# Short runs of extra matmuls at TensorE's longest waits, in a two-block transformer kernel on one core

## What is computed

```python
# mixer of layer 1 ("stick"): 16 heads, per query block
z = einsum('bhqd,bhkd->bhqk', qb, kb) * scale
log_stay  = where(causal, log_sigmoid(-z), 0.0)
log_after = cumsum(log_stay, axis=3, reverse=True) - log_stay
weights   = where(causal, exp(log_sigmoid(z) + log_after), 0.0)
out       = einsum('bhqk,bhkd->bhqd', weights, vb)

# second block, per layer; mixer 0 is NSA (three branches: compressed,
# selected, window), mixer 1 is forgetting attention ("fox")
h = rms_norm_2(x, norm_g[i, 0])
m = nsa_mixer(h, ...) if i == 0 else fox_mixer(h, ...)
x = x + rms_norm_2(m, norm_g[i, 1])                                  # post norm
h = rms_norm_2(x, norm_g[i, 2])
x = x + rms_norm_2(squared_relu_mlp(h, w_up[i], w_down[i]), norm_g[i, 3])  # post norm
```

## Time and profile before

| | |
|---|---|
| three runs | 1797.10, 1798.36 and 1802.62 us; median 1798.36 us |
| profiled execution, first to last instruction | 1802.1 us |
| TensorE busy | 1713.9 us, 95% of that span |
| VectorE, ScalarE, GpSimd busy | 1078.2, 789.6, 193.4 us |
| mean TensorE clock granted | 0.970 of 2.4 GHz |
| read from HBM | 280 MB, 156 GB/s over the span |
| chain of work that ended last | TensorE 86%, VectorE 6%, ScalarE 4% of the span |

### The profile page before, as it was taken

The page is one execution under the profiler, slowest core; times in us unless marked ns, Lnnn a source line. Parts: engine busy times, 40 slices in busy tenths (PEclk is TensorE's granted clock), DMA queues, the critical chain, the costliest instruction groups (busy, mean ns, idle before and its releaser), DMA issues.

```text
span 1802.1 us, 30970 instructions
## 1 busy us (share of the span) xinstructions
PE 1713.9 (95%) x13150; PEld 1644.2 (91%) x13150; DVE 1078.2 (60%) x1034; ACT 789.6 (44%) x903; POOL 193.4 (11%) x141
## 2 busy tenths in 40 slices
PE   7999998999999999999999999888999899789997
PEld 7999985899999999989999988677999898679997
DVE  7555776465567655676556776555655565456553
ACT  6343466444345434454344434434444443344441
POOL 1000123200002000120001351212000011120000
PEclk9999999999999999999999998789999999899999
DMA  7554451264453554455544442011655343125540
GB/s 294 187 187 162 176 201 44 74 237 183 167 187 149 202 210 164 163 201 191 209 164 163 183 178 94 24 57 68 227 178 176 136 164 140 71 76 205 186 163 24
DMA packets 39631, 282.26 MB, mean 157 GB/s; under 512 B 4416, under 2 KB 4544, under 8 KB 5760
## 3 DMA queue, kind: packets, MB, share of 16 engines
q1 hardware_dynamic: 39168, 279.59, 41.9%
q0 software_dynamic: 384, 1.51, 0.2%
HBM read 280.03 MB, written 1.05 MB: 156 GB/s over the span
## 4 chain that ended last, share of the span: by engine, by line
PE 86%; DVE 6%; ACT 4%; DMA 1%; POOL 1%; issue 1%; POOLq 0%; SPq 0%; ACTq 0%; DVEq 0%
PE ps L326 26%; PE ps L327 26%; PE ps L328 26%; DMA raw<-weights 1%; DVE hT_lo L1181 1%; ACT arena L1031 1%; ACT w_hi L873 1%; PE ps L656 1%; DVE w_lo L1169 1%; PE ps L600 1%; PE ps L408 1%; DVE arena L1273 1%; PE ps L613 1%; PE ps L632 0%; PE ps L657 0%
## 5 line engine op out<-in xcount | busy, mean ns | idle before, releaser
L326 PE MATMUL ps<-hT_hi,w_hi 128*128 128x256 f32 x2520 | 722.7, 287 | 32.0 <-DVE hT_lo L1181 26.2
L327 PE MATMUL ps<-hT_lo,w_hi 128*128 128x256 f32 x2520 | 717.1, 285 | 0.0
L328 PE MATMUL ps<-hT_hi,w_lo 128*128 128x256 f32 x2520 | 716.8, 284 | 0.0
L1169 DVE TENSOR_TENSOR w_lo<-raw,w_hi 128x2048 fp32r<-128x2048 f32 x264 | 600.6, 2299 | 136.7 <-ACT w_hi L873 136.6
L873 ACT ACTIVATE w_hi<-raw 128x2048 fp32r<-128x2048 f32 x264 | 494.8, 1902 | 67.2 <-DMA raw<-weights 67.1
L326 PEld LDWEIGHTS ps<-hT_hi,w_hi 128*128 128x128 f32 x2520 | 487.2, 193 | 36.1 <-issue 16.8
L327 PEld LDWEIGHTS ps<-hT_lo,w_hi 128*128 128x128 f32 x2520 | 488.1, 194 | 0.8 <-issue 0.7
L328 PEld LDWEIGHTS ps<-hT_hi,w_lo 128*128 128x128 f32 x2520 | 487.8, 194 | 0.0
L326 PE MATMUL ps<-hid_hi,w_hi 128*128 128x256 f32 x1256 | 355.7, 283 | 2.1 <-DVE hid_lo L1237 2.1
L327 PE MATMUL ps<-hid_lo,w_hi 128*128 128x256 f32 x1256 | 356.6, 284 | 0.0
L328 PE MATMUL ps<-hid_hi,w_lo 128*128 128x256 f32 x1256 | 351.6, 280 | 0.0
(11 more groups left out here) (222 smaller groups left out, 1451.8 us busy)
## 6 DMA issues: line engine op xcount, KB each, us to landing
raw<-weights SPq DMA_DIRECT2D x264, 1024.0 KB, 4.8
X<-x SPq DMA_DIRECT2D x2, 512.0 KB, 7.0
out<-X SPq DMA_DIRECT2D x4, 256.0 KB, 2.0
arena<-p POOLq DMA_DIRECT2D x2, 256.0 KB, 5.4
arena<-counts POOLq DMA_DIRECT2D x1, 512.0 KB, 5.3
arena<-nsa_tables POOLq DMA_DIRECT2D x1, 448.0 KB, 7.0
const<-constants SPq DMA_DIRECT2D x1, 423.0 KB, 9.7
cols<-parameters SPq DMA_DIRECT2D x1, 213.5 KB, 2.6
```

Of the source, the lines that this page charges most:

```text
L326: nc.tensor.matmul(dst, a_hi, b_hi, start=start, stop=False, skip_group_check=True)
L327: nc.tensor.matmul(dst, a_hi, b_lo, start=False, stop=False, skip_group_check=True)
L328: return nc.tensor.matmul(dst, a_lo, b_hi, start=False, stop=stop, skip_group_check=True)
L1169: nc.vector.tensor_tensor(unit_cols(w_lo, u, 0, UNIT), raw[:, r * UNIT:(r + 1) * UNIT], f(unit_cols(w_hi, u, 0, UNIT)), ALU.subtract).then ...
```

## The change

A helper `keep_clock(n, b)` issues n matmuls of 128 x 512 from `hid_hi` into bank b. Their result is read by nobody, and no semaphore counts them. It is called

- behind `spread(3)` in `post_norm`: 16 into bank 1, four times in the program;
- ahead of the wait of `weighted(g)` in stick: 14 into bank 7 for g = 0, 8 into bank 0 for g = 1 and 2, 4 into bank 0 for g = 3;
- ahead of the wait for the transposed weights in NSA's `weighted(n)` of each cmp job: 8 into bank 4;
- in `compress`, behind the wait for bank 2 and ahead of that for the hidden values: 8 into bank 2.

That is 64 + 34 + 32 + 8 = 138 matmuls. Since bank 0 is written now, the wait for `z_used`, which was not needed before, stands ahead of weighted(1).

```diff
+            def keep_clock(n, b):
+                for _ in range(n):
+                    nc.tensor.matmul(bank(b), hid_hi[:, 0:P], hid_hi[:, 0:512], start=True, stop=True, skip_group_check=True)
...
             def post_norm(first):
                 sum_squares(range(first, 4), 3)
                 spread(3)
+                keep_clock(16, 1)
...
                 def weighted(g):
+                    if g:
+                        keep_clock(8 if g < GROUPS - 1 else 4, 0)
+                    else:
+                        keep_clock(14, 7)
                     pe.wait_ge(*w_ready.due(me))
...
                 for n in range(GROUPS):
+                    if n == 1:
+                        pe.wait_ge(*z_used.due(me))
                     weighted(n)
                     if n + 2 < GROUPS:
                         after(n + 2)
-                z_used.due(me)
                 project(u0 + 12)
...
+                    if br == "cmp":
+                        keep_clock(8, 4)
                     pe.wait_ge(*tA_done.due(me))
...
                 def compress():
                     pe.wait_ge(*s_used.due(me))
+                    keep_clock(8, 2)
                     pe.wait_ge(*hid_cmp.due(me))
```

## The result

| | before | changed |
|---|---|---|
| runs | 20 | 20 |
| median | 1799.28 us | 1805.59 us |
| lowest to highest | 1796.75 to 1807.94 us | 1801.96 to 1807.49 us |

The ratio of the two is 1.0026, with a 95% interval of 1.0017 to 1.0034: 3 to 6 us slower, where 0.0 was forecast. It is not the quotient of the medians, which lie 6.3 us apart; it stands for 4.7 us. That is inside the 0.3% that the prediction called no measurable change, but only by the width of this 0.3%: the interval leaves 1 out, and the median lies 1.1 us above the upper end of the predicted range. The kernel became slightly slower, and the sum that gave 0.0 did not see it.

The account below looks back on a forecast made before the run. TensorE was busy 95% of the span, so time at 1.2 GHz on the path was in question. Terms -0.7, 0, -0.4, -0.8, +0.8, +1.4, 0 and -0.3 summed to 0.0: 1798.4 us forecast, range 1790.5 to 1804.5.

Parts of the forecast that it names:

- Falls that move: NSA's cmp jobs: clock falls move to new waits, 0 to +1.4 us for each of three head groups, taken +0.8 in all.
- Job 5, -0.8: NSA's cmp job 5: 2.3 us of its wait stay empty; bounds 0 and -2.5 us, taken -0.8.
- the surest term: NSA's job 11: added matmuls delay the weighted sum that project needs, +1.4 us on the path, +3.2 at 1.2 GHz.
- Stick, -0.7: Stick: after(3) may lose up to 3.7 us, weighted(3) win up to 1.4; taken +0.7 and -1.4, so -0.7.
- Compress, 0: NSA's compress: gain goes into job 0's wait and 11 us at clock 0.50 stay; 0, or up to -5 us.
- the post norms, 0, 0, 0 and -0.3: Behind NSA, fox and the last post norm 0; behind the first MLP bounds 0 and -1.4 us, taken -0.3.
- The price of a matmul: Each added matmul: 0.23 us from start to start at 2.4 GHz, at most 0.46 at 1.2 GHz.
- the clock holds in every wait up to 3.3 us: Rival, chance 0.19: gains in stick, jobs 2, 5, 8 and fox, less job 11, sum to -7.1 us, so 1791.3.
- the added matmuls run at 1.2 GHz: Rival, chance 0.11: also the clock falls ahead of after(3); +9.5 us less 1.4 for weighted(3), about 1806.5.

Follow-up runs that it names:

- before again: The kernel before, unchanged, run once more against the kernel before: 1799.39 us beside 1798.69, ratio 1.0010.
- the filled NSA kernel: Kernel before plus all of the change's NSA matmuls and ten more ahead of each of weighted(3), (6) and (9): 1799.20 us beside 1799.33, ratio 1.0000.
- with NSA filled the part as made: Kernel before plus NSA's matmuls without job 11's, ten ahead of weighted(3), (6), (9), and stick's 14, 8, 8, 4: 1796.59 us beside 1798.67.
- the whole change with both fills: The whole change plus ten matmuls ahead of each of weighted(3), (6), (9) and twelve ahead of after(3): 1796.24 us beside 1799.07 before, ratio 0.9987.
- the fastest kernel: Kernel before plus NSA's matmuls without job 11's, stick's matmuls, ten ahead of weighted(3), (6), (9), twelve ahead of after(3): 1795.19 us beside 1799.07.
- the stick kernel with its fill: Kernel before plus stick's 14, 8, 8 and 4 matmuls and twelve more ahead of after(3): 1802.86 us beside 1799.33, ratio 1.0012.
- the kernel without the stick part: Kernel before plus NSA's matmuls without job 11's, and ten ahead of each of weighted(3), (6) and (9): 1797.63 us beside 1799.07, ratio 0.9994.

## Why the prediction was off, by its own steps

**Falls that move: the step that failed.** The mechanism was forecast and is there: a wait of about 3 us without matmuls ahead of weighted(3) and weighted(9), with the clock at 0.50 behind it. Its price was set at +0.8 us for three head groups. Against before again they cost 1.64, 1.65 and 1.76 us on the path; two of them win 0.14 and 0.15 ahead of it, so 4.8 net. NSA as a whole grew by 6.1 us (102.2 to 108.3), which with 1.3 for job 11 leaves the same 4.8. The kernel with these matmuls alone measured +3.3, against -0.4 for the same terms in the sum (-0.4 - 0.8 + 0.8). The bound of +1.4 for each fell short by 0.2 to 0.4, since it counted the weighted sum alone, and the clock stays down over the first transposes behind it; the value taken in it was far too small. The row on which I costed it is only a part of the reason. In that execution of before, weighted(3) stood at 1.2 GHz nearly to its end, where in before again half of its work runs at full speed. But even against that execution weighted(3) and (9) cost 1.27 and 1.47 us more with the change, and (6) 0.48 less: +2.3 in all, and not +0.8.

**Job 5, -0.8.** In the profile of before the clock was down from 1158.2 to 1171.8, over weighted(6), and against it the change does win 1.05 us from weighted(5) to (6) (8.37 to 7.32). In before again the clock was back at 1163.6, and that distance is 7.30: there was nothing to win.

**The base.** I knew that the profiled span lay 3.7 us over the median (5.6, with the 1.9 between a span and its run's time), subtracted that, and went on reading its rows as if the surplus lay evenly. It lay in NSA, at the place that the change touches: half of the 7.5 us from the first scores to weighted(1), where the clock was down for 17 us and not 10.2, and 3.2 us around weighted(6). The page's row of the clock, too, shows 7 or 8 only in NSA's slices and one of fox, not at stick and the post norms, as the prediction has it.

**Job 11, "the surest term", +1.4.** In the trace the weighted sum follows the transposes' start by 2.2 us and not by 0.9, so +1.3. It is 1.3 again in the trace of the kernel with job 11's alone. That kernel measured +0.7, with an interval of 0.9996 to 1.0018 that holds both 0 and 1.4; leaving it out took 1.6 us from the filled NSA kernel (1799.20 to 1797.63, in two series). The size is borne out, not more.

**Stick, -0.7.** By itself +2.5, which looked like a failed step. But its section was no longer than in before again (33.4, 33.7 and 32.1 us from after(1)'s last matmuls to `project` in the three traces that have it as made, against 33.8), and with NSA filled the part as made measured 2.1 us under before, where the kernel without it measured 1.4 under: -0.7, with intervals of two us on either side this doesn't confirm the forecast, but it makes +2.5 as a cost of its own unlikely. The two halves are as costed: after(3) lost (5.9 us against 3.67; in the kernel before run again, which had a fall there too, 5.3), weighted(3) won (from 3.6 to 2.2 us). One of the prediction's signs of being wrong, after(3) near 6 us, thus came. Here too the profile was of the rarer kind: of the eight traces in which stick is unchanged, six have after(3) at 5.2 to 6.7 us and a section of 33.4 to 33.8, and two, that profile among them, 3.67 us and 31.6 to 31.8. So the sum charged the change with a fall that most executions had already. Where the 2.5 us of the stick part alone were lost, its one trace does not show: it is of one of the fastest executions (1797.73 us), with 102.3 us for NSA.

**Compress, 0, and the post norms, 0, 0, 0 and -0.3.** Right against before again: the gain of compress went whole into job 0's wait, and from the first scores to weighted(2) it is 33.7 us with the change and 33.8 in before again. But the 11 us at 0.50 did not stay, as the prediction had it; the clock was down for 3.4 us there, and against the profile of before that distance shrank by 3.7. Behind NSA's post norm the gain went into the wait for POOL's squares, 1.56 where about 1.7 was forecast. Behind the first MLP the clock fell between the chunks, as feared. From `spread(3)` to the next stage's `spread(7)` it is 19.7 us behind NSA and fox and 22.4 behind the first MLP, in before again and with the post norms' matmuls alone: nothing was won. The four together measured +0.3.

**The price of a matmul** was 0.23 us, as forecast: sixteen take 3.90 us and eight 2.11, so that eight more take 1.8. A whole set takes 0.2 to 0.6 us more than its number times 0.23, as its row reaches from the first start to the last modelled end. At 1.2 GHz, where one set ran in the whole change with both fills, eight took 3.78 us, 0.43 from start to start, where at most 0.46 was forecast.

**The rivals.** That the clock holds in every wait up to 3.3 us is ruled out by the windows. That the added matmuls run at 1.2 GHz is ruled out too at stick, jobs 2 and 11, though its other half, the fall ahead of after(3), came true, and its time of 1806.5 lies nearest to the 1805.59 measured. It came there for another reason.

**What stays open.** Why NSA takes its longer course more often after the stick part is not shown. The runs show two groups of times, one trace of before in each, and a lower granted clock in the upper one. That the shorter stick moves NSA against whatever times the clock's changes is an inference from these; no execution of the stick kernels from the upper group was profiled. Nor does the difference simply go once NSA's waits are filled: NSA with its next waits filled still spreads from 1796.1 to 1804.6 us, and in the trace of the fastest kernel NSA began 4.5 us earlier than in that of the kernel without the stick part (1093.31 and 1097.80) and took 4.9 us longer (106.15 and 101.28). A second cause stands beside the clock and was not tested, a transfer. In the stick kernel with its fill NSA began 4.5 us earlier than in before again and ended only 1.8 earlier, in an execution of the lower group; 2.0 of the 2.7 us lie ahead of job 0's transposes, and there the last weights to be rounded ahead of NSA's masks came 1.3 us later, counted from NSA's first scores (ScalarE's rows, first the stick kernel with its fill, whose first scores are at 1093.41, then before again, at 1097.95):

```profile
1093.78 1.91 ACT L862 ACTIVATE w_hi<-raw 128x2048 fp32r<-128x2048 f32 x1 [5.07 <-DMA raw<-weights]
```

```profile
1096.98 1.91 ACT L873 ACTIVATE w_hi<-raw 128x2048 fp32r<-128x2048 f32 x1 [3.70 <-DMA raw<-weights]
```

## What to carry to other kernels

Matmuls that only keep the clock were worth little here in one wait alone: most of what they win lengthens the next wait of the same engine, and the clock may fall there, perhaps ahead of work that had run at full speed. Follow the gain to the next empty wait, fill that too, and leave out those that stand on the path; here this turned +0.26% into -0.22%. And before a term of 1 us is read from one trace, see where in the spread of its runs the profiled execution lies: one that is 4 us over the median has them somewhere, and perhaps just there.

## What the runs showed that was not expected

The same program differs in itself by 7.5 us in NSA alone (102.2 and 109.7 us from first scores to `project`), with the same instructions and nearly the same waits, by where the clock falls: at compress and job 0 it is 0.50 from 1105.6 to 1115.8 us in the one, and in the other from 1103.6 to 1120.6, 17 us, of which the earlier trace rows has the last 11, this row the first 3.5, and job 0's wait lies between them:

```profile
1103.60:1107.10 3.50, 3.50 (x16) 3.34 (x16) 3.40 (x7) 2.23 (x12) 0.09 (x1) 0.50 0.00 0
```

A wait's own length did not decide it: the clock fell in one of 1.72 us, and the wait of 2.11 us at job 5 left it up in some traces and was followed by a fall in others.
